# Three late expert groups instead of two in a decoder block, and a value stage written out with its weight splitting moved from GpSimd to ScalarE and VectorE

## The chip, the core and the metric

The kernel runs on one NeuronCore of a Trainium2 chip. The metric is the device time of one execution in microseconds; the median of three executions stands for a kernel. The traces are of one profiled execution.

## What is computed

A hybrid decoder block for 256 tokens of width 2048 in float32: two gated token mixers, a cross-attention to 256 memory tokens, and a product-key expert layer (PEER), with residual sums between them. The change touches only the last of these and its routing:

```python
def peer_ffn(xn, wq, sub_keys, u_tab, v_tab):
    q = (xn @ wq).reshape(B, S, PEER_HEADS, 2, PEER_HALF)
    s = jnp.einsum('bshpd,hpnd->bshpn', q, sub_keys)
    top_v, top_i = lax.top_k(s, PEER_TOPK)                 # 16 of 128, two halves
    cand = top_v[..., 0, :, None] + top_v[..., 1, None, :]  # 256 candidates
    cand_v, cand_i = lax.top_k(cand, PEER_TOPK)
    experts = i1 * PEER_NKEYS + i2                          # 16 of 16,384
    gates = jax.nn.softmax(cand_v, axis=-1)
    ...
    act = jax.nn.gelu(jnp.einsum('td,tkd->tk', xb, u_tab[eb]))
    return jnp.einsum('tk,tkd->td', gb * act, v_tab[eb])
```

There are 8 heads and 16 experts for each head and token; both tables have 16,384 rows of 2048 floats (134 MB each). The output is the final RMSNorm of the sum.

## The kernel before

The kernel is written in Bass, with one hand-written instruction stream for each engine, and semaphores between them. After the projections (up to about 1578 us of the profiled execution) the expert layer follows in three stages.

**The gather stage.** A *group* is one head for 128 tokens, so there are 16 groups (`GROUPS`); groups 0 to 7 are of the first 128 tokens. For a group VectorE first runs `route(g)`: top 16 of two rows of 128 scores, top 16 of their 256 sums, the expert numbers (`idx_all`) and the gates; ScalarE takes the exponent (`gate_exp`). GpSimd then gathers for each of the 16 experts one row of `peer_u` per token with an indirect DMA (128 x 2048 floats, 1.05 MB) into a ring of 8 (`gather_rows`), VectorE multiplies it with the token and sums (`dot_rows`, one instruction per expert), ScalarE takes the gelu (`expert_gelu`) and VectorE the product with the gate (`weigh`), which gives `w_all`. VectorE runs this as a loop: dots of group g, route of group g+3, weigh of g. In before the loop runs over g = 1 to 12, and group 13 follows alone.

**Spreading.** The output could be had by gathering `peer_v` too. The kernel rather reads the whole table once: it builds the dense matrix `spread` (16,384 experts x 256 tokens) from the weights, one *unit* of four tokens at a time (64 units): a marking of the expert's row (`row_hot`) times a marking of its column (`col_ring`) on TensorE. ScalarE builds the markings of units 0 to 31 during the gather stage (`make_unit`) and copies the product out (`copy_unit`); for units 32 to 63 VectorE makes the row marks (`mark_rows`) and GpSimd most column marks, after the last group has been weighed.

**The value stage.** 256 *steps*, each a half row block of `peer_v` (128 x 1024 floats, 0.52 MB, `v_raw`, four buffers, loaded by SyncE's queue). ScalarE rounds it to `v_hi` (two buffers), VectorE makes the rest `v_lo` (two buffers), and TensorE multiplies in 12 matmuls of 512 columns: 8 with `v_hi` (by `e_hi` and `e_lo`), then 4 with `v_lo`. `e_hi` and `e_lo` are the same split of a *batch* of `spread`, good for 8 steps; 32 batches. In before GpSimd makes them from batch 1 on (`split_weights`: a copy and a subtraction). All 12 matmuls of a step wait for `v_split`, that is for the step's `v_lo`.

**Late groups.** Some groups of the second 128 tokens are left out of `spread` (`LATE`, groups 14 and 15). Their rows of `peer_u` and `peer_v` are gathered during the value stage by GpSimd into two buffers (`late_row`); VectorE dots the 16 `u` rows and adds the 16 weighted `v` rows to `late_sum`, one row after every third step from step 32 to step 224; TensorE adds `late_sum` near the end.

Each engine runs its own code in order; what it waits for is written out as `wait_ge` on a semaphore. The names `Apart` and `Chain` are helpers for such waits; in a loop the value waited for is computed in a register.

## Time and profile before

| | |
|---|---|
| median of three executions | 3069.42 us (3069.34 to 3070.61) |
| the profiled execution | 3075.78 us, of it the span of instructions 3074.1 us |
| gather stage, 1578 to 2243 us | VectorE busy 47 of 50 us, TensorE clock 0.50 |
| spreading of units 32 to 63 | 2244 to 2297 us |
| value stage | 2303 to 3062 us; TensorE busy 47 of 50 us, VectorE 37, GpSimd 18 |
| TensorE, VectorE, ScalarE, GpSimd busy over the whole | 77%, 69%, 42%, 25% |

The times of the profiled execution are microseconds from its first instruction. The busy time of an engine in a window says how much of it the engine worked, PEclk is the granted TensorE clock (1.00 is 2.4 GHz), the DMA share is the mean busy share of the 16 DMA engines. A row of a timeline gives start, length, engine, line of the kernel, operation, and after it the idle time ahead and who ended it. The profiled execution took 6.4 us more than the median.

### The profile page before, as it was taken

To read this page: it belongs to the slowest core of one execution; us is meant where nothing else is said; L and a number is where in the kernel's file an instruction comes from. 1 tells how busy PE (TensorE), PEld (TensorE's weight loads), DVE (VectorE), ACT (ScalarE), POOL (GpSimd) and SP (SyncE) were. 2 spreads that over 40 slices of the span, in tenths; PEclk is the share of its full clock that TensorE was granted. 3 is DMA by queue.
4 is the path that set the end of the run, shared out by engine and by line. 5 is a ranking of instruction groups with operands and counts; after the bars stand their busy time and mean duration, and the time that the engine had idled before them with its cause. 6 is when DMAs were issued, how large, how long until landed. Compare 5 with 4: busy or idle time off the path is not lost. (4 is left out here: it accounts for less than half of the span.)

```text
span 3074.1 us, 44560 instructions
## 1 busy us (share of the span) xinstructions
PE 2367.7 (77%) x15833; PEld 2184.1 (71%) x15833; DVE 2112.0 (69%) x2724; ACT 1284.0 (42%) x1857; POOL 756.8 (25%) x461
## 2 busy tenths in 40 slices
PE   7999999999999999989870000122259999999998
PEld 6899999999999999989860000012248777777776
DVE  6774556666456446434589999999975777777764
ACT  4554444444444344433520000377873333333333
POOL 0000000000001001000045756656662333433320
PEclk8999999999999999999885555555589999999999
DMA  6453665445655555535467989989815887888865
GB/s 199 130 159 117 190 181 154 148 149 164 200 165 177 184 178 177 180 110 184 146 260 325 368 342 380 367 345 377 338 37 178 298 292 283 287 288 296 296 233 170
DMA packets 338990, 695.74 MB, mean 226 GB/s; under 512 B 24792, under 2 KB 266672, under 8 KB 301376
## 3 DMA queue, kind: packets, MB, share of 16 engines
q1 hardware_dynamic: 296080, 386.19, 39.8%
q0 software_dynamic: 42304, 307.25, 24.9%
q8 instruction: 69, 1.13, 0.2%
q10 hardware_dynamic: 496, 0.84, 0.1%
q14 instruction: 41, 0.34, 0.0%
HBM read 692.11 MB, written 2.10 MB: 226 GB/s over the span
## 5 line engine op out<-in xcount | busy, mean ns | idle before, releaser
L357 DVE TENSOR_TENSOR b_w_lo<-b_raw,b_w_hi 128x1024 fp32r<-128x1024 f32 x464 | 570.0, 1245 | 534.0 <-ACT b_w_hi L352 533.4
L352 ACT ACTIVATE b_w_hi<-b_raw 128x1024 fp32r<-128x1024 f32 x464 | 485.1, 1057 | 615.9 <-PE bank L375 609.3
L375 PE MATMUL bank<-b_act_hi,b_w_hi 128*128 128x256 f32 x1920 | 548.7, 286 | 12.1 <-DVE b_w_lo L357 9.2
L375 PE MATMUL bank<-b_act_lo,b_w_hi 128*128 128x256 f32 x1920 | 545.3, 284 | 0.0
L375 PE MATMUL bank<-b_act_hi,b_w_lo 128*128 128x256 f32 x1920 | 545.2, 284 | 0.0
L1886 DVE TENSOR_TENSOR b_v_lo<-b_v_raw,b_v_hi 128x1024 fp32r<-128x1024 f32 x256 | 365.9, 1435 | 237.1 <-ACT b_v_hi L1065 216.8
L1864 DVE CUSTOM_DVE_ANT_0 b_u_ring<-b_u_ring,b_xnN 128x2048 f32<-128x2048 f32 x220 | 488.5, 2286 | 5.9 <-issue 4.1
L1065 ACT ACTIVATE b_v_hi<-b_v_raw 128x1024 fp32r<-128x1024 f32 x256 | 271.6, 1061 | 484.9 <-PE bank L1452 453.5
L642 POOL DMA_INDIRECT b_u_ring<-in_peer_u,b_stage_idx x220 | 399.6, 1817 | 228.9 <-DVE b_dots L1864 155.2
L375 PEld LDWEIGHTS bank<-b_act_hi,b_w_hi 128*128 128x128 f32 x1920 | 370.6, 193 | 15.6 <-DVE b_w_lo L357 7.8
L375 PEld LDWEIGHTS bank<-b_act_lo,b_w_hi 128*128 128x128 f32 x1920 | 370.7, 193 | 0.1
L375 PEld LDWEIGHTS bank<-b_act_hi,b_w_lo 128*128 128x128 f32 x1920 | 370.5, 193 | 0.0
L375 PE MATMUL bank<-b_att_hi,b_w_hi 128*128 128x256 f32 x1280 | 365.3, 285 | 4.1 <-DVE b_att_lo L460 4.1
L375 PE MATMUL bank<-b_att_hi,b_w_lo 128*128 128x256 f32 x1280 | 363.9, 284 | 0.0
L375 PE MATMUL bank<-b_att_lo,b_w_hi 128*128 128x256 f32 x1280 | 363.9, 284 | 0.0
L1452 PE MATMUL bank<-b_v_hi,b_e_hi 128*128 128x512 f32 x1024 | 327.0, 401 | 36.6 <-DVE b_v_lo L1886 30.3
L1452 PE MATMUL bank<-b_v_hi,b_e_lo 128*128 128x512 f32 x1024 | 322.3, 396 | 0.0
L1411 PE MATMUL bank<-b_consts,b_isel_all 128*128 128x128 f32 x4 | 1.4, 442 | 374.3 <-DVE b_w_all L1870 373.0
L1452 PE MATMUL bank<-b_v_lo,b_e_hi 128*128 128x512 f32 x1024 | 276.2, 392 | 0.0
L1411 PEld LDWEIGHTS bank<-b_consts,b_isel_all 128*128 128x128 f32 x4 | 0.6, 204 | 375.4 <-DVE b_w_all L1870 373.8
L1452 PEld LDWEIGHTS bank<-b_v_hi,b_e_hi 128*128 128x128 f32 x1024 | 191.8, 191 | 94.6 <-DVE b_v_lo L1886 50.9
L375 PEld LDWEIGHTS bank<-b_att_hi,b_w_hi 128*128 128x128 f32 x1280 | 247.7, 193 | 5.0 <-issue 5.0
(307 smaller groups left out, 3879.5 us busy)
## 6 DMA issues: line engine op xcount, KB each, us to landing
b_v_raw<-in_peer_v SPq DMA_DIRECT2D x256, 512.0 KB, 4.7
b_raw<-in_w_in SPq DMA_DIRECT2D x208, 512.0 KB, 3.9
b_raw<-in_w_proj_dsa SPq DMA_DIRECT2D x32, 512.0 KB, 3.9
b_raw<-in_w_proj_gla SPq DMA_DIRECT2D x32, 512.0 KB, 3.5
b_raw<-in_w_xk SPq DMA_DIRECT2D x32, 512.0 KB, 4.4
b_raw<-in_w_out SPq DMA_DIRECT2D x32, 512.0 KB, 3.4
b_raw<-in_w_xv SPq DMA_DIRECT2D x32, 512.0 KB, 4.6
b_raw<-in_w_xq SPq DMA_DIRECT2D x32, 512.0 KB, 4.4
```

What stands on the lines that cost most here:

```text
L352: act.activation(w_hi[:, q], raw[:, UQ * c + q], ACT.Copy).then_inc(w_high, 1)
L357: dve.tensor_tensor(w_lo[:, q], raw[:, UQ * c + q], w_hi[:, q].bitcast(F32), ALU.subtract).then_inc(w_split, 1)
L375: mm = pe.matmul(proj[c][:, n], lhs, rhs, start=(q == 0 and n == 0 and k == 0 and t == 0), stop=(q == UQ - 1 and k == UK - 1 and t == 2), ...
L642: pool.indirect_dma_start(row_tile(k, early), None, u_rows, bass.IndirectOffsetOnAxis(ap=stage_idx[:, slot, k:k + 1], axis=0)).then_inc(u_ ...
L1065: act.activation(v_hi[:, n % 2], v_raw[n % 4], ACT.Copy).then_inc(sem("v_high"), 1)
L1411: mm = pe.transpose(bank[0][:, k * P:(k + 1) * P], src[:, t * P:(t + 1) * P], ident)
L1452: mm = pe.matmul(bank[4 * t + 2 * v + m], e[:, slot, i, t * P:(t + 1) * P], x[:, v, m * 512:(m + 1) * 512], start=False, stop=(last and n ...
L1864: dve.tensor_tensor_reduce(u, u, xnN[:, t], 1.0, 0.0, ALU.mult, ALU.add, dots[:, k:k + 1]).then_inc(sem("dotted"), 1)
L1886: dve.tensor_tensor(v_lo[:, n % 2], v_raw[n % 4], v_hi[:, n % 2].bitcast(F32), ALU.subtract).then_inc(sem("v_split"), 1)
```

## The change

It does seven things (the diff below has GpSimd, ScalarE, TensorE and VectorE in this order). (1) `LATE` holds three groups, 13 to 15; so the gather stage has 13 groups, and 96 late rows (48 of each table) are spread over steps 24 to 235, at distances of two or three steps (`late_at`). (2) The loops of the gather stage are written out, so that each wait is on a constant; `route` reads `sims` itself and the copy `sc` is gone; GpSimd's index copies (`stage_idx`) are gone. (3) Since the loop over g now ends at 11, `route(14)` and `route(15)` both run at g = 11. (4) ScalarE makes the marks of units 0 to 3 ahead, in groups 5 and 6 (`row_ahead`, `mark_unit`), before their weights are known; at g = 7 it then finishes 8 units. (5) ScalarE makes `e_hi` and VectorE `e_lo` for all batches; GpSimd only gathers in the value stage. (6) TensorE waits for `v_high` ahead of a step's 8 products with `v_hi`, and for `v_split` only ahead of the 4 with `v_lo`; `v_lo` has four buffers; ScalarE in turn waits that `v_lo` of two steps ago is made. (7) ScalarE's and VectorE's value stage is written out, with the late rows inside; `late_dots` and a clearing of `late_sum` are gone.

```diff
-LATE = (GROUPS - 2, GROUPS - 1)
+LATE = tuple(range(GROUPS - 3, GROUPS))
 EARLY = LATE[0]
-LATE_UNIT = 32
+STEPS = 2 * NKEYS
+PER_BATCH = 2 * BATCH
+LATE_ROWS = 2 * PTOP * len(LATE)
+LATE_STEP = 24
+MADE_AHEAD = 4
...
+    def late_at(n):
+        span = STEPS - 2 * PER_BATCH - LATE_STEP - 4
+        return [m for m in range(LATE_ROWS) if LATE_STEP + span * m // LATE_ROWS == n]
...
-        pool.wait_ge(sem("spread_copied"), UNITS)
-        first = LATE_UNIT // (2 * BATCH)
-        for b in range(1, first + 1):
-            split_weights(b, b % 2)
...
+        pool.wait_ge(sem("e_split"), 4)
+        for m in range(LATE_ROWS):
+            g, kind, k = LATE[m // (2 * PTOP)], m // PTOP % 2, m % PTOP
+            if m >= 2:
+                pool.wait_ge(sem("late_used"), m - 1)
+            pool.indirect_dma_start(late_row[m % 2], None, (u_rows, a["peer_v"][0])[kind],
+                                    bass.IndirectOffsetOnAxis(ap=idx_all[:, g * PTOP + k:g * PTOP + k + 1], axis=0)
+                                    ).then_inc(sem(f"late_landed{m % 2}"), 16)
...
+        def value_high(n):
+            act.wait_ge(v_landed[n % 4], n // 4 * 16 + 16)
+            if n >= 2:
+                act.wait_ge(sem("v_high_used"), n - 1)
+                act.wait_ge(sem("v_split"), n - 1)
+            act.activation(v_hi[:, n % 2], v_raw[n % 4], ACT.Copy).then_inc(sem("v_high"), 1)
+        def weights_high(b):
+            if b >= 2:
+                act.wait_ge(sem("v_used"), PER_BATCH * (b - 1))
+            hi, w = weights_of(b, e_hi)
+            act.activation(hi, w, ACT.Copy).then_inc(sem("e_high"), 1)
...
+            if g == EARLY - 2:
+                for late in range(g + 4, GROUPS):
+                    gate_exp(late)
-            for u in range(made, min(made + (4 if g == 7 else 6), UNITS // 2)):
+            for u in range(made, min(made + (MADE_AHEAD + 4 if g == 7 else 6), UNITS // 2)):
...
+        for n in range(STEPS):
+            value_high(n)
+            if n == 1:
+                weights_high(0)
+            if n % PER_BATCH == 2 and n // PER_BATCH + 1 < NKEYS // BATCH:
+                weights_high(n // PER_BATCH + 1)
...
-                pe.wait_ge(sem("v_split"), b * 4 * BATCH + n + 1)
+                pe.wait_ge(sem("v_high"), b * 4 * BATCH + n + 1)
                 slot, i, v = n // (2 * BATCH), n // 2 % BATCH, n % 2
-                for parts, x, done in (((e_hi, e_lo), v_hi, "v_high_used"), ((e_hi,), v_lo, "v_used")):
+                for parts, x, done in (((e_hi, e_lo), v_hi[:, v], "v_high_used"), ((e_hi,), v_lo[n % 4], "v_used")):
+                    if done == "v_used":
+                        pe.wait_ge(sem("v_split"), b * 4 * BATCH + n + 1)
...
-            link(dve.tensor_copy(sc, sims[:, bass.ds(g, 1)].rearrange("p g s n -> p (g s) n")))
-            top16(*[(tv[:, s], ti[:, s], sc[:, s], sc2[:, s]) for s in range(2)])
+            top16(*[(tv[:, s], ti[:, s], sims[:, g, s], sc2[:, s]) for s in range(2)])
...
+        for n in range(STEPS):
+            value_low(n)
+            if n == 1:
+                weights_low(0)
+            if n % PER_BATCH == 3 and n // PER_BATCH + 1 < NKEYS // BATCH:
+                weights_low(n // PER_BATCH + 1)
+            for m in late_at(n):
+                late_step(m)
```

GpSimd's program in the value stage of before, from the fifth batch on; `b_late_row` is the gathered row, `b_e_hi` and `b_e_lo` the split weights:

```order
L675 CAST b_e_hi<-b_spread 128x1024
L677 TENSOR_TENSOR b_e_lo<-b_spread,b_e_hi 128x1024
L697 DMA b_late_row_117<-in_peer_u,b_stage_idx 128x2048
L697 DMA b_late_row_118<-in_peer_u,b_stage_idx 128x2048
L675 CAST b_e_hi<-b_spread 128x1024
L677 TENSOR_TENSOR b_e_lo<-b_spread,b_e_hi 128x1024
```

The same place after the change, from the last column marks on:

```order
L664 TENSOR_SCALAR b_col_ring<-b_consts,b_turned 128x128 x72
L679 DMA b_late_row_116<-in_peer_u,b_idx_all 128x2048
L679 DMA b_late_row_117<-in_peer_u,b_idx_all 128x2048
L679 DMA b_late_row_116<-in_peer_u,b_idx_all 128x2048
L679 DMA b_late_row_117<-in_peer_u,b_idx_all 128x2048
```

Both kinds of splitting instruction have left GpSimd, and its stream holds nothing but the 96 row gathers.

VectorE in before, the loop body of the late `u` rows; `b_v_lo` is the remainder of a step's values, the two L1898 rows are one dot and its sum's read-out:

```order
L1886 TENSOR_TENSOR b_v_lo<-b_v_raw_125,b_v_hi 128x1024
L1898 ISA b_late_row_117,b_late_dots<-b_late_row_117,b_xnN 128x2048
L1898 ISA b_late_dots 128x1
L1883 REGISTER_ALU
L1886 TENSOR_TENSOR b_v_lo<-b_v_raw_126,b_v_hi 128x1024
L1883 REGISTER_ALU
L1886 TENSOR_TENSOR b_v_lo<-b_v_raw_127,b_v_hi 128x1024
L1883 REGISTER_ALU
L1886 TENSOR_TENSOR b_v_lo<-b_v_raw_128,b_v_hi 128x1024
```

VectorE after the change, from step 24 on:

```order
L1886 TENSOR_TENSOR b_v_lo_130<-b_v_raw_125,b_v_hi 128x1024
L1902 ISA b_late_row_116,b_dots<-b_late_row_116,b_xnN 128x2048
L1902 ISA b_dots 128x1
L1886 TENSOR_TENSOR b_v_lo_131<-b_v_raw_126,b_v_hi 128x1024
L1886 TENSOR_TENSOR b_v_lo_132<-b_v_raw_127,b_v_hi 128x1024
L1902 ISA b_late_row_117,b_dots<-b_late_row_117,b_xnN 128x2048
L1902 ISA b_dots 128x1
L1886 TENSOR_TENSOR b_v_lo_133<-b_v_raw_128,b_v_hi 128x1024
L1891 TENSOR_TENSOR b_e_lo<-b_spread,b_e_hi 128x1024
```

A row comes after every second step (every fifth distance or so is three), and the batch's `b_e_lo` has joined the stream once in 8 steps.

ScalarE after the change, at g = 11, the last turn in which it builds units:

```order
L1044 ACTIVATE b_gelu<-b_dots 128x16
L990 ACT_TABLE_LOAD
L990 ACTIVATE b_egate,b_stat<-b_cv,b_stat 128x16 x2
L1005 ACTIVATE b_row_hot<-b_consts,b_turned 128x128 x4
L1005 ACTIVATE b_col_ring<-b_consts,b_turned 128x128 x4
```

Where before had one exponent ahead of the last six units, there are two now, of groups 14 and 15, and the second waits for `route(15)`.

## Rows read from the trace of the kernel before

**Rows 1.** windows, a gather and a value stretch; first row: columns

```profile
core 0: us, PE busy (x) PEld busy (x) DVE busy (x) ACT busy (x) POOL busy (x), PEclk, DMA share, GB/s
1850.00:1900.00 50.00, 0.00 (x0) 0.00 (x0) 47.34 (x76) 3.18 (x5) 32.58 (x18) 0.50 0.89 358
2600.00:2650.00 50.00, 46.94 (x198) 37.73 (x197) 37.42 (x22) 17.79 (x17) 17.96 (x9) 0.97 0.84 306
```

**Rows 2.** timeline, VectorE, one gather turn: start, length (us), engine, line

```profile
1909.58 0.29 DVE L1838 COPY b_sc<-b_sims 128x256 f32 x1
...
1921.48 2.29 DVE L1864 CUSTOM_DVE_ANT_0 b_u_ring<-b_u_ring,b_xnN 128x2048 f32<-128x2048 f32 x1 [0.41 <-issue]
...
1956.89 0.28 DVE L1838 COPY b_sc<-b_sims 128x256 f32 x1
```

**Rows 3.** timeline, VectorE, route(0) outside the loop, first and last instruction

```profile
1537.71 0.29 DVE L1838 COPY b_sc<-b_sims 128x256 f32<-128x256 f32 x1
...
1547.04 0.23 DVE L1858 TENSOR_SCALAR b_gates_all<-b_egate,b_stat 128x16 f32<-128x16 f32 x1
```

**Rows 4.** timeline, the end of the gather stage, VectorE and ScalarE

```profile
2193.03 0.29 DVE L1838 COPY b_sc<-b_sims 128x256 f32 x1
...
2200.00 0.31 ACT L1010 ACTIVATE b_egate<-b_cv,b_stat 128x16 f32<-128x16 f32 x1 [5.34 <-DVE b_stat L1845]
...
2242.78 0.21 ACT L1057 ACTIVATE b_gelu<-b_dots 128x16 f32<-128x16 f32 x1
...
2243.03 0.17 DVE L1870 TENSOR_TENSOR b_w_all<-b_gelu,b_gates_all 128x16 f32<-128x16 f32 x1 [2.99 <-ACT b_gelu L1057]
```

**Rows 5.** timeline, the start of the value stage, VectorE and TensorE

```profile
2297.51 4.58 DVE L1886 TENSOR_TENSOR b_v_lo<-b_v_raw,b_v_hi 128x1024 fp32r<-128x1024 f32 x2 [3.22 <-ACT b_v_hi L1065]
...
2303.28 1.22 PE L1452 MATMUL bank<-b_v_hi,b_e_hi 128*128 128x512 f32 x2 [4.62 <-DVE b_e_lo L1943]
```

**Rows 6.** timeline, one even step of the value stage, three engines

```profile
2313.97 0.61 PE L1452 MATMUL bank<-b_v_hi,b_e_hi 128*128 128x512 f32 x2
...
2315.79 1.07 PE L1452 MATMUL bank<-b_v_lo,b_e_hi 128*128 128x512 f32 x4
...
2316.05 1.06 ACT L1065 ACTIVATE b_v_hi<-b_v_raw 128x1024 fp32r<-128x1024 f32 x1 [1.66 <-PE bank L1452]
...
2316.69 0.61 PE L1452 MATMUL bank<-b_v_hi,b_e_hi 128*128 128x512 f32 x2
...
2317.14 1.23 DVE L1886 TENSOR_TENSOR b_v_lo<-b_v_raw,b_v_hi 128x1024 fp32r<-128x1024 f32 x1 [1.50 <-ACT b_v_hi L1065]
```

**Rows 7.** timeline, a step in which GpSimd splits weights

```profile
2328.92 3.26 POOL L677 TENSOR_TENSOR b_e_lo<-b_spread,b_e_hi 128x1024 fp32r<-128x1024 f32 x1
...
2330.74 2.53 DVE L1886 TENSOR_TENSOR b_v_lo<-b_v_raw,b_v_hi 128x1024 fp32r<-128x1024 f32 x1 [0.82 <-ACT b_v_hi L1065]
```

**Rows 8.** groups, 2310:3040: count, busy us, mean ns, idle before

```profile
L1886 DVE TENSOR_TENSOR b_v_lo<-b_v_raw,b_v_hi 128x1024 fp32r<-128x1024 f32 x247 | 352.7, 1434 | 223.4 <-ACT b_v_hi L1065 203.1 <-PE bank L1452 19.8 <-DVE b_w_all L1870 0.3
```

**Rows 9.** the chain that ended last, its end: start us, length us

```profile
3015.34 3.43 PE bank L1476 x8
...
3062.34 1.84 ACT b_hN L1120 x6
```

**Rows 10.** windows of the value stage; columns as in rows 1

```profile
2312.00:2326.00 14.00, 14.00 (x64) 11.58 (x63) 6.53 (x6) 5.30 (x5) 0.00 (x0) 1.00 0.59 190
...
2400.00:2500.00 100.00, 93.86 (x400) 75.24 (x399) 74.69 (x59) 35.78 (x34) 38.35 (x20) 0.98 0.81 295
...
2525.00:2530.00 5.00, 5.00 (x24) 4.14 (x23) 4.05 (x4) 1.98 (x2) 0.34 (x1) 1.00 1.01 416
```

**Rows 11.** tile b_late_row, 2300:3040: instructions and time from issue to landing

```profile
L1902 DVE SCALAR_TENSOR_TENSOR b_late_sum<-b_late_row,b_w_all,b_late_sum x32: 2339/2346/4492, 2536.8 to 2961.4; 128x2048 f32<-128x2048 f32 x32
...
DMA to landing us min/median/max: 8.1/8.6/10.7
```

**Rows 12.** tile b_v_raw, 2400:2900: time from issue to landing

```profile
DMA to landing us min/median/max: 3.5/5.7/9.0
```

More of the change, by code:

```diff
@@ L273, in hybrid_block @@
     v_hi = sb("v_hi", [2, VCOLS], SCR, F32R)
-    v_lo = sb("v_lo", [2, VCOLS], SCR + 8 * K, F32R)
+    v_lo = [sb(f"v_lo{n}", [VCOLS], at, F32R) for n, at in enumerate((SCR + 8 * K, SCR + 12 * K, WRK, WRK + 4 * K))]
     gfin = sb("gfin", [D], HT)
@@ L700, in _ @@
-        for b in range(first + 25, NKEYS // BATCH):
-            split_weights(b, b % 2)
+        pool.wait_ge(sem("e_split"), 4)
[6 more added lines that the diff above has]
+                                    ).then_inc(sem(f"late_landed{m % 2}"), 16)
@@ L1057, in expert_gelu @@
             act.activation(gelu, dots, ACT.Gelu_apprx_tanh).then_inc(sem("gelu_ready"), 1)
-        def values_high(at, steps, first=False):
-            for n in steps:
-                act.wait_ge(v_landed[n % 4], at * 16 + (n // 4 + 1) * 16)
-                if not (first and n < 2):
-                    act.wait_ge(sem("v_high_used"), at * 4 + (n - 1))
-                act.activation(v_hi[:, n % 2], v_raw[n % 4], ACT.Copy).then_inc(sem("v_high"), 1)
+        def value_high(n):
[9 more added lines that the diff above has]
+            act.activation(hi, w, ACT.Copy).then_inc(sem("e_high"), 1)
         peer_pair(PQ, 0)
@@ L1075, in _ @@
         gate_exp(3)
-        with act.Fori(1, 8) as g:
+        for g in range(1, 8):
             expert_gelu(g)
             gate_exp(g + 3)
-        turn_over(0, (0, 3))
+            if g == 4:
+                act.wait_ge(sem("routed"), PEER_H)
+                turn_over(0, (0, 2))
+            if g in (5, 6):
+                mark_unit(2 * (g - 5))
+                mark_unit(2 * (g - 5) + 1)
+        turn_over(1, (2, 3))
         made = 0
@@ L1088, in _ @@
         copy_unit(UNITS // 2 - 1)
-        turn_over(1, (0, 2))
+        turn_over(2, (0, 2))
         act.wait_ge(sem("routed"), GROUPS)
@@ L1452, in values @@
                                 mm = pe.matmul(bank[4 * t + 2 * v + m], e[:, slot, i, t * P:(t + 1) * P],
-                                               x[:, v, m * 512:(m + 1) * 512], start=False,
-                                               stop=(last and n >= 4 * BATCH - 2 and x is v_lo), skip_group_check=True)
+                                               x[:, m * 512:(m + 1) * 512], start=False,
+                                               stop=(last and n >= 4 * BATCH - 2 and done == "v_used"), skip_group_check=True)
                     mm.then_inc(sem(done), 1)
@@ L1469, in _ @@
         pe.wait_ge(sem("spread_copied"), UNITS)
-        seed(range(2))
-        values(0, first=True)
-        with pe.Fori(1, NKEYS // (2 * BATCH) - 1) as b:
+        seed(range(2)).then_inc(sem("seeded"), 1)
+        with pe.Fori(0, NKEYS // (2 * BATCH) - 1) as b:
             values(b)
-        pe.wait_ge(sem("late_used"), 4 * PTOP)
+        pe.wait_ge(sem("late_used"), LATE_ROWS)
         for n in range(4):
@@ new lines, in value_low, with weights_low @@
+        def value_low(n):
+            dve.wait_ge(sem("v_high"), n + 1)
+            if n == 2:
+                dve.wait_ge(sem("seeded"), 2)
+            if n >= 4:
+                dve.wait_ge(sem("v_used"), n - 3)
+            dve.tensor_tensor(v_lo[n % 4], v_raw[n % 4], v_hi[:, n % 2].bitcast(F32), ALU.subtract).then_inc(sem("v_split"), 1)
+        def weights_low(b):
+            dve.wait_ge(sem("e_high"), b + 1)
+            hi, w = weights_of(b, e_hi)
+            dve.tensor_tensor(weights_of(b, e_lo)[0], w, hi.bitcast(F32), ALU.subtract).then_inc(sem("e_split"), 1)
@@ new lines, in late_step @@
+        def late_step(m):
+            g, kind, k = LATE[m // (2 * PTOP)], m // PTOP % 2, m % PTOP
+            row = late_row[m % 2]
+            if kind == 1 and k == 0:
+                weigh(g)
+                dve.wait_ge(sem("weights_ready"), g + 1)
+            dve.wait_ge(sem(f"late_landed{m % 2}"), m // 2 * 16 + 16)
+            if kind == 0:
+                dve.tensor_tensor_reduce(row, row, xnN[:, 1], 1.0, 0.0, ALU.mult, ALU.add, dots[:, k:k + 1]
+                                         ).then_inc(sem("late_used"), 1)
+                return
+            w = w_all[:, g * PTOP + k:g * PTOP + k + 1]
+            dve.wait_ge(sem("late_used"), m)
+            if m == PTOP:
+                dve.wait_ge(sem("e_split"), 8)
+                dve.tensor_scalar(late_sum, row, w, None, ALU.mult).then_inc(sem("late_used"), 1)
+            else:
+                dve.scalar_tensor_tensor(out=late_sum, in0=row, scalar=w, in1=late_sum, op0=ALU.mult, op1=ALU.add
+                                         ).then_inc(sem("late_used"), 1)
```

182 lines of the change are left out of this document (51 added, 131 removed).

## The prediction

> **What bounds the kernel now.** I read the busy windows first, to see which engine is full in which stage. In the gather stage VectorE works 47.3 of 50 us and TensorE nothing; in the value stage TensorE works 46.9 of 50 at nearly the full clock (0.97), VectorE 37.4, and the DMA engines 0.84 [rows 1]. So a VectorE instruction counts in full in the first, and only what keeps TensorE waiting counts in the second. Nothing before 1578 us is touched.
>
> The timeline of the gather stage gives the price of a turn: from one `COPY b_sc` to the next 47.3 us, of them 11.9 up to the first dot (`route`, `weigh`, the branch) and 35.4 for 16 dots, 2.21 us each [rows 2]. `route(0)`, which stands outside the loop, took 9.56 us for the same instructions [rows 3]: the loop's waits on register values cost the rest. The end of the stage is not VectorE's: its last `weigh` waited 2.99 us for ScalarE's gelu [rows 4].
>
> The value stage runs from TensorE's first product at 2303.3 [rows 5] to ScalarE's first reading of the results at 3062.3 [rows 9], 759.1 us. An even step takes 2.72 us (2313.97 to 2316.69) [rows 6]. 256 of them are 696.3; `late_sum` adds 3.4 [rows 9]; the first step runs at half pace (1.22 us for two matmuls against 0.61) and costs 2.7 more [rows 5, 6]. That makes 702.4, so TensorE loses 56.7 us to waits. The cause is in the timeline: `v_lo` takes 1.23 us alone, but 2.53 beside GpSimd's `TENSOR_TENSOR` of 3.26 us [rows 6, 7]; its mean is 1.43 over 247 [rows 8], and single late-row instructions of 2.35 us take up to 4.49 [rows 11]. All 12 matmuls of a step wait for it. In the even step `v_lo` is ready at 2318.37, and its step starts at 2319.41 (2316.69 plus 2.72): 1.0 us of slack, less than one contended instruction or one late row takes.
>
> **The change, part by part.**
>
> *Gather stage.* The 16 dots stay at 35.4 us. `route` loses the copy (0.29 us and its wait, 0.32) and runs like the one outside the loop: 9.24. With some 0.25 for `weigh` a turn is 44.9 instead of 47.3. The dots of group 12 ended at 2193.1; the last dots ahead of the same work are now those of group 11. That is one turn less (47.3) and ten turns each 2.4 shorter (24.0): 71.3 us earlier. Behind this point it gets longer. ScalarE's exponent stood at 2200.0, and from there its six units, eight column marks and the gelu ran without a gap to 2243.0, 43.0 us [rows 4]. Now two exponents stand ahead of the units, and the second waits for `route(15)`: 9.5 for `route(14)` and `weigh`, then 5.9 into `route(15)`: 15.4 us after the dots, where it was 6.9. VectorE itself would be done after 9.5 + 9.3 + 35.4 = 54.2 us, ScalarE after 15.4 + 43.0 = 58.4, against 49.9 before: 8.5 given back. The copies of `route(2)` and `route(3)` add 0.6. Net **63.4 us saved**. The marks made ahead I cost at nothing: ScalarE has 3.18 us of work in 50 in that stretch [rows 1], and in turn 7, where it now finishes eight units, it needs no longer than the 35 us of dots. Without them, turn 7 would have four full units more and ScalarE would be late by part of them.
>
> Is there another floor for the gather turn? 16 rows of 1.05 MB at the 358 GB/s of now are 46.9 us, but DMA is busy only 0.89 of the time [rows 1]; at its full pace (358/0.89 = 402) they take 41.8, under 44.9. So VectorE stays the bound, with less room.
>
> *Spreading.* Its instructions and waits stay, offset by the gelu: 0.
>
> *Start of the value stage.* The first two `v_lo` took 4.58 us beside GpSimd's split; alone they take 2.46 [rows 5, 6]. TensorE waited for what follows them: **2.1 us saved**.
>
> *Value stage.* GpSimd's splits go, so the contention goes. VectorE gets 31 more subtractions of 1.23 us and 32 more rows. In steps 24 to 235 (212 steps, 96 rows, 2.21 steps apart) its work for a step is 1.23 + 2.35/2.21 + 1.23/8 = 2.45 us of 2.72: full to 90%, yet under. What it is late by has more room: `v_lo` is now wanted only ahead of the last four matmuls, 1.81 us into the step (2313.97 to 2315.79) [rows 6], so the slack is 1.04 + 1.81 = 2.9 us. A row (2.35) fits; a row and a weight subtraction in one step put the next `v_lo` 2.1 us behind its place, and it still fits. ScalarE's extra `e_hi` (about 1.06 once in 8 steps) lies in its idle 1.66 us a step. If VectorE and ScalarE keep up, the whole 56.7 us of waits vanish. That is the one bound: nothing lost, step 2.72.
>
> The other bound is transfers. A step in that stretch moves 0.524 MB of values and 1.049/2.21 = 0.475 MB of rows, 0.999 MB in 2.72 us: 367 GB/s, where the stage now averages 295 at a DMA share of 0.81. In time: values alone hold the share at 0.59, so 1.60 us a step; the average of now (a step of 0.874 MB at 295 GB/s is 2.96 us, 0.81 of it 2.40) leaves (2.40 - 1.60) x 3 = 2.4 us a row [rows 10]. The new step needs 1.60 + 2.4/2.21 = 2.69 us of DMA in 2.72. A 5-us window in which 416 GB/s were reached in this very mix says there is a little more to have [rows 10]. The second sign is the ring of two rows: issue to use may take 2 x 2.21 x 2.72 = 12.0 us less 2.35 for the row itself and some 0.3 for waking GpSimd: 9.4 us. The landing takes 8.6 in the median, 10.7 at most [rows 11]. At 10.7 for every row the step would be (10.7 + 2.65)/4.42 = 3.02 us. A value block has four buffers, 10.9 us, of which 2.4 go for its two splits; it lands in 5.7, at most 9.0 [rows 12], and ScalarE has 2.3 us of slack beside.
>
> So the step in the late stretch lies between 2.72 and 3.02 us, 0 to 64 us over 212 steps. I take 2.80, nearer to the lower end since every mean fits and only the tails do not: **17 us given back**.
>
> At this place the Trainium skill speaks against the change: "DMA: Bandwidth & Descriptors", section "Where 436 GB/s comes from", holds that transfers from HBM are bound by some 358 GB/s per core. The 416 GB/s window and the 402 above go beyond that here. By the page the late step would be an estimated 0.999 MB / 358 GB/s = 2.79 us and the give-back 15 us; by the window's 416 it would be 2.72 and nothing.
>
> *Sum.* 63.4 + 2.1 + 56.7 - 17 = 105.2 us. The profiled execution took 3075.8 and would take 2970.6. It lies 6.4 above the median, which I carry over: **2964 us** for the median, 3.4% less.
>
> **The rivals.**
>
> *A: transfers set the pace of the late stretch.* For it: 2.69 of 2.72 us of DMA, a row ring with 0.8 us to spare over the median, and instructions that wait in order, so a late row holds up the next `v_lo`. Against it: no late row has made VectorE wait so far (the waits ahead of `v_lo` are for ScalarE and TensorE [rows 8]). Step 2.88 to 3.1, at 2.96 (the pace the stage has now): 51 us given back instead of 17, 2998 us.
>
> *B: GpSimd isn't what slows `v_lo`, or VectorE becomes the bound.* If `v_lo` kept its mean of 1.43, VectorE's step would be 2.65, with waking times some 2.85: 28 us given back, 2975. Against it: 1.23 us in every step without a GpSimd split.
>
> *C: slower than before.* If the 295 GB/s of now were already what this mix of queues yields, the step would be 0.999/295 = 3.39 us, 142 us lost in the late stretch against 2.72: 3089 us. It decides from a step of about 3.30 on, or a row landing of 11.9 us. Against it: windows of 416 and shares of 0.81, which leave idle time.
>
> *D: the gather stage gives less.* If the written-out turns kept 47.3 us (the extra time being no matter of register waits), 24 us and a little more would be missing: 2989.
>
> **How the numbers follow.** The forecast (late step 2.72 to 2.88, 2947 to 2981 us) gets 0.60, B falls in its range and gets 0.06 of its own, A 0.24, D 0.05, C 0.03, and 0.02 is for what I have not seen. The low end is the stage without any give-back, 2947, less 3 for small terms; the high end reaches over most of A and D: 2944 to 3000. A measurement of this kernel tells 0.2% (6 us) from no change. All cases but C end far below: faster 0.96, within 0.2% 0.01, slower 0.03.
>
> **What would show it.** Right: dots of group 12 begin 18.8 us after those of group 11 end, with gather turns of 44.9; ScalarE's gelu ends 4 us after VectorE's last dot; `v_lo` has a mean near 1.23; even steps of 2.72 before step 24 and after 235, and 2.75 to 2.85 between; the DMA share there over 0.93. Wrong: idle time of VectorE ahead of late rows, rows landing in over 9.4 us, ScalarE waiting for value blocks; turns over 46 us; or gaps for code that is now written out instead of looped.

## The result: 2.4% faster, at the far end of the range

| | before | after |
|---|---|---|
| median | 3070.02 us (4 runs, 3069.34 to 3075.49) | 2999.31 us (4 runs, 2990.09 to 3006.46) |
| ratio, 95% interval | | 0.9764 [0.9734, 0.9794] |
| the profiled execution | 3075.78 us | 3006.46 us |

The forecast was 2964 us, range 2944 to 3000. Sign and range hold, but the time is 35 us above the forecast and close to that of rival A (2998), in part by luck, as told below. One later execution of the changed kernel took 7326 us and enters no figure. The profiled execution of the changed kernel is the slowest of its four, 7.2 us above their median; that of before lay 6.4 above the median on which the forecast was built. The table takes both profiled executions apart in the terms of the forecast's sum. The gelu is the last one of the gather stage, the value stage is from TensorE's first product to the end of its last.

| | before | after | saved | forecast |
|---|---|---|---|---|
| gather stage, to the gelu's end | 2242.99 | 2188.11 | 54.9 | 63.4 |
| from there to the first product | 60.3 | 58.2 | 2.1 | 2.1 |
| value stage | 759.0 | 746.5 | 12.5 | 56.7 - 17 = 39.7 |
| sum | | | 69.5 | 105.2 |

The executions differ by 69.3 us, so nothing is missing. Two terms of the forecast's sum are off: the gather stage by 8.5 us, the value stage by 27.2.

### The gather stage after

VectorE's timeline (start, length, engine, line, operation), with the first and the last dot of group 11, the exponents and units of ScalarE behind it, and the last weigh; they answer to [rows 2, 4]:

```profile
2083.06 2.29 DVE L1863 CUSTOM_DVE_ANT_0 b_u_ring<-b_u_ring,b_xnN 128x2048 f32<-128x2048 f32 x1
...
2118.46 0.08 DVE L1863 DVE_READ_ACCUMULATOR2_ANT b_dots<- 128x1 f32 x1
...
2124.43 0.31 ACT L990 ACTIVATE b_egate<-b_cv,b_stat 128x16 f32<-128x16 f32 x1 [4.34 <-DVE b_stat L1844]
2133.80 0.31 ACT L990 ACTIVATE b_egate<-b_cv,b_stat 128x16 f32<-128x16 f32 x1 [8.96 <-DVE b_stat L1844]
2134.10 1.26 ACT L1005 ACTIVATE b_row_hot<-b_consts,b_turned 128x128 f32<-128x128 f32 x4
...
2139.78 1.25 ACT L1005 ACTIVATE b_row_hot<-b_consts,b_turned 128x128 f32<-128x128 f32 x4
...
2162.39 1.23 ACT L1005 ACTIVATE b_row_hot<-b_consts,b_turned 128x128 f32<-128x128 f32 x4
...
2187.89 0.22 ACT L1044 ACTIVATE b_gelu<-b_dots 128x16 f32<-128x16 f32 x1
2188.14 0.18 DVE L1869 TENSOR_TENSOR b_w_all<-b_gelu,b_gates_all 128x16 f32<-128x16 f32 x1 [15.55 <-ACT b_gelu L1044]
```

Group 11's dots end at 2118.5, where those of group 12 ended at 2193.1: 74.6 us earlier, 71.9 forecast. The second exponent begins 15.3 us behind them (15.4 worked out). But from there to the gelu it is 54.1 us and not 43.0, and VectorE stands for 15.55 us. On ScalarE a unit begins with four `b_row_hot` instructions; one begins every 5.65 us, and between 2134.10 and 2162.39 six of them do. The same place of before, the start of each unit behind the exponent of 2200.0 in [rows 4]:

```profile
2200.31 1.26 ACT L1025 ACTIVATE b_row_hot<-b_consts,b_turned 128x128 f32<-128x128 f32 x4
...
2205.96 1.24 ACT L1025 ACTIVATE b_row_hot<-b_consts,b_turned 128x128 f32<-128x128 f32 x4
...
2211.62 1.23 ACT L1025 ACTIVATE b_row_hot<-b_consts,b_turned 128x128 f32<-128x128 f32 x4
...
2217.26 1.25 ACT L1025 ACTIVATE b_row_hot<-b_consts,b_turned 128x128 f32<-128x128 f32 x4
```

There were four units in before. The prediction took them for six.

### The value stage after

Windows of the value stage (columns as in [rows 1]): before the late rows, between them, and the whole late stretch; the second answers to [rows 10]:

```profile
2252.00:2300.00 48.00, 48.00 (x214) 39.74 (x213) 24.65 (x21) 20.97 (x21) 0.00 (x0) 1.00 0.57 187
2400.00:2500.00 100.00, 95.62 (x407) 74.77 (x406) 76.22 (x55) 39.29 (x39) 25.19 (x15) 1.00 0.92 334
2304.00:2920.00 616.00, 592.69 (x2528) 469.86 (x2528) 486.20 (x382) 247.34 (x239) 162.28 (x94) 1.00 0.93 339
```

Before the late rows begin TensorE has no gap. Among them the DMA share is 0.93 at 339 GB/s, and TensorE is idle for 23.3 us by this view (the last section tells why the loss is larger than that). The groups of VectorE and the waits in the same window (total, times, longest), which answer to [rows 8, 11], and the landing time of the value blocks, which answers to [rows 12]:

```profile
L1886 DVE TENSOR_TENSOR b_v_lo<-b_v_raw,b_v_hi 128x1024 fp32r<-128x1024 f32 x211 | 252.2, 1220 | 60.7 <-ACT b_v_hi L1052 60.7
L1902 DVE CUSTOM_DVE_ANT_0 b_late_row<-b_late_row,b_xnN 128x2048 f32<-128x2048 f32 x48 | 109.9, 2289 | 36.9 <-DMA b_late_row<-in_peer_u,b_idx_all 36.6
L1911 DVE SCALAR_TENSOR_TENSOR b_late_sum<-b_late_row,b_w_all,b_late_sum 128x2048 f32<-128x2048 f32 x45 | 105.7, 2349 | 33.3 <-DMA b_late_row<-in_peer_v,b_idx_all 32.0 <-issue 1.3
```

```profile
ACT b_v_hi L1052 <- DMA b_v_raw<-in_peer_v: 290.4, 136, 4.9
...
PEld bank L1451 <- DVE b_v_lo L1886: 40.6, 54, 2.5
DVE b_late_row L1902 <- DMA b_late_row<-in_peer_u,b_idx_all: 36.6, 25, 2.9
DVE b_late_sum L1911 <- DMA b_late_row<-in_peer_v,b_idx_all: 32.0, 23, 3.7
PE bank L1451 <- DVE b_v_lo L1886: 20.0, 29, 2.1
```

```profile
DMA to landing us min/median/max: 6.1/7.9/9.2
```

The contention with GpSimd is gone: `v_lo` takes 1.22 us on the mean (1.43 before), a row never more than 2.36. What waits now waits for DMA: ScalarE for value blocks 136 times, VectorE for rows 48 times (68.6 us). One place of VectorE's and TensorE's timelines shows how a late row reaches TensorE:

```profile
2644.99 2.35 DVE L1911 SCALAR_TENSOR_TENSOR b_late_sum<-b_late_row,b_w_all,b_late_sum 128x2048 f32<-128x2048 f32 x1 [3.65 <-DMA b_late_row<-in_peer_v,b_idx_all]
2647.26 2.35 DVE L1886 TENSOR_TENSOR b_v_lo<-b_v_raw,b_v_hi 128x1024 fp32r<-128x1024 f32 x2
```

```profile
2645.81 0.61 PE L1451 MATMUL bank<-b_v_hi,b_e_lo 128*128 128x512 f32 x2
2648.53 1.49 PE L1451 MATMUL bank<-b_v_lo,b_e_hi 128*128 128x512 f32 x4 [2.11 <-DVE b_v_lo L1886]
2649.82 1.06 PE L1451 MATMUL bank<-b_v_hi,b_e_hi 128*128 128x512 f32 x2
2650.68 1.06 PE L1451 MATMUL bank<-b_v_hi,b_e_lo 128*128 128x512 f32 x2
```

VectorE stands 3.65 us for a row, the `v_lo` behind it comes late, TensorE stands 2.11 us, and its next products take 1.06 us a pair where they took 0.61.

### The profile page after: what moved, and what is told of

The parts are those of the page before. It is cut to its first block, busy times and chain, and to the rows that moved or that the text cites. A ratio compares the mean times of both kernels' runs of the same rounds, so it can differ in the third digit from the quotient of the medians.

```text
span 3004.7 us, 43116 instructions
## 1 busy us (share of the span) xinstructions
PE 2362.4 (79%) x15833; PEld 2173.8 (72%) x15833; DVE 2097.8 (70%) x2746; ACT 1309.9 (44%) x1887; POOL 635.2 (21%) x399
## 4 chain that ended last, share of the span: by engine, by line
PE 54%; DVE 24%; DMA 13%; issue 5%; ACT 4%; POOL 1%; DVEq 0%; SPq 0%; ACTq 0%; POOLq 0%
PE bank L377 42%; DVE b_u_ring L1863 13%; PE bank L1451 6%; DMA b_v_raw<-in_peer_v 5%; DMA b_late_row<-in_peer_v,b_idx_all 4%; DMA b_late_row<-in_peer_u,b_idx_all 4%; DVE b_v_lo L1886 1%; DVE b_late_sum L1911 1%; PE bank L1261 1%; PE bank L1146 1%; ACT b_spread L996 1%; ACT b_v_hi L1052 1%; DVE b_w_lo L359 1%; DVE b_rstd L421 1%; PE bank L1428 1%
## 5 line engine op out<-in xcount | busy, mean ns | idle before, releaser
L1863 DVE CUSTOM_DVE_ANT_0 b_u_ring<-b_u_ring,b_xnN 128x2048 f32<-128x2048 f32 x204 | 453.0, 2288 | 1.6 <-DMA b_u_ring<-in_peer_u,b_idx_all 1.5
L653 POOL DMA_INDIRECT b_u_ring<-in_peer_u,b_idx_all x204 | 385.3, 1888 | 245.6 <-DVE b_dots L1863 132.6
L1886 DVE TENSOR_TENSOR b_v_lo<-b_v_raw,b_v_hi 128x1024 fp32r<-128x1024 f32 x256 | 307.1, 1221 | 122.8 <-ACT b_v_hi L1052 122.8
L1451 PE MATMUL bank<-b_v_hi,b_e_hi 128*128 128x512 f32 x1024 | 320.2, 394 | 5.5 <-DVE b_e_lo L1891 2.7
L377 PEld LDWEIGHTS bank<-b_att_lo,b_w_hi 128*128 128x128 f32 x1280 | 247.5, 193 | 0.1
L377 PEld LDWEIGHTS bank<-b_att_hi,b_w_lo 128*128 128x128 f32 x1280 | 247.5, 193 | 0.0
L1451 PEld LDWEIGHTS bank<-b_v_lo,b_e_hi 128*128 128x128 f32 x1024 | 188.0, 188 | 78.7 <-DVE b_v_lo L1886 42.2
```

What stands on the lines that cost most here:

```text
L377: mm = pe.matmul(proj[c][:, n], lhs, rhs, start=(q == 0 and n == 0 and k == 0 and t == 0), stop=(q == UQ - 1 and k == UK - 1 and t == 2), ...
L653: pool.indirect_dma_start(row_tile(k, g == 0), None, u_rows, bass.IndirectOffsetOnAxis(ap=idx_all[:, at:at + 1], axis=0)).then_inc(u_lande ...
L1451: mm = pe.matmul(bank[4 * t + 2 * v + m], e[:, slot, i, t * P:(t + 1) * P], x[:, m * 512:(m + 1) * 512], start=False, stop=(last and n >= ...
L1863: dve.tensor_tensor_reduce(u, u, xnN[:, t], 1.0, 0.0, ALU.mult, ALU.add, dots[:, k:k + 1]).then_inc(sem("dotted"), 1)
L1886: dve.tensor_tensor(v_lo[n % 4], v_raw[n % 4], v_hi[:, n % 2].bitcast(F32), ALU.subtract).then_inc(sem("v_split"), 1)
```

## The experiments

All are edits of the changed kernel. The value stage's floor below is what e1 and e2 reach, where TensorE has no gap: 701.7 us. "Stage" is the value stage, always from the first product to the end of the last. The three columns of events are each from one profiled execution, which may lie some 7 us off the median of its kernel; medians and ratios to before are from all runs.

| | late groups | last gelu | first product | stage | median | ratio to before |
|---|---|---|---|---|---|---|
| after, again | 3 | 2184.6 | 2244.4 | 748.0 | 3003.7 | 0.9756 [0.9741, 0.9772] |
| e1 | 2 | 2208.7 | 2267.4 | 701.7 | 2982.6 | 0.9698 [0.9685, 0.9711] |
| e2 small rows | 3 | 2184.1 | 2242.1 | 701.7 | 2957.2 | 0.9623 [0.9606, 0.9641] |
| e3 larger ring | 3 | 2181.9 | 2240.7 | 722.1 | 2976.6 | 0.9691 [0.9678, 0.9704] |
| e4 rows to 248 | 3 | 2188.7 | 2247.1 | 717.9 | 2974.5 | 0.9675 [0.9661, 0.9688] |
| e5 tail | 3 | 2171.1 | 2232.1 | 739.3 | 2985.8 | 0.9728 [0.9715, 0.9742] |
| e8 = e3+e4+e5 | 3 | 2171.2 | 2232.1 | 708.5 | 2956.7 | 0.9632 [0.9619, 0.9646] |
| e6 GpSimd splits | 2 | 2208.5 | 2267.4 | 707.6 | 2986.5 | 0.9721 [0.9706, 0.9736] |
| e7 one wait | 2 | 2207.3 | 2265.9 | 711.3 | 2989.2 | 0.9731 [0.9716, 0.9746] |
| e10 = e6+e7 | 2 | 2208.3 | 2267.6 | 748.1 | 3029.0 | 0.9853 [0.9839, 0.9868] |
| e11 = e10, 2 buffers | 2 | 2204.8 | 2264.7 | 751.9 | 3027.5 | 0.9849 [0.9834, 0.9863] |

**The changed kernel again.** 

> The changed kernel once more, since its four times lie between 2990 and 3006 us while e3, e4 and e5 each came with one of their own: median 2990 to 3000 us, and a value stage of 735 to 747 us in the profiled execution. If it is below 2990, the gains put to e3, e4 and e5 against the first profile are too large by the difference.

Both came out a little above what was expected: median 3003.7 (five times between 2993.6 and 3006.1), stage 748.0, which is that of the first profile within 1.5 us. So the gains of e3, e4 and e5 against the first profile aren't overstated. The gelu moved by 3.3 us with the same instructions, so a few us of the column "last gelu" mean nothing: the last gelu of e3 is 6 us earlier than that of after though e3 changes nothing ahead of it. The gains below are therefore read from the stage, and from the gap between two events of one trace, and held against the medians.

**Two groups (e1).** What does the third late group bring?

```diff
-LATE = tuple(range(GROUPS - 3, GROUPS))
+LATE = tuple(range(GROUPS - 2, GROUPS))
```

> Two late groups (14 and 15) as before, all else as after the change: 64 late rows over the same 212 steps. The gather stage gets one more turn of 44.8 us on VectorE, but ScalarE then has fewer units left behind the last group: the profile of after has six units of 5.65 us and a gelu 15.6 us later than VectorE's last dot, and here I expect no such wait, so the gelu comes some 20 us later than in after, near 2208. Theory of transfers (some 340 GB/s is what value blocks and rows together get): 64 rows in 212 steps ask for 0.30 rows a step and 309 GB/s at 2.72 us a step, so the value stage falls from 746.5 to about 705 to 712 us, and the sum is about 15 to 20 us faster than after. Theory of lock step (a row is asked for only when one of two buffers is free, and VectorE, ScalarE and TensorE wait for each other at each late row, whatever the bandwidth): the loss goes by the number of rows, 64 of 96, so the value stage is about 731 us and the sum is some 5 us slower than after.

The window of the late stretch (TensorE busy for all of it):

```profile
2304.00:2920.00 616.00, 616.00 (x2720) 510.06 (x2719) 444.70 (x353) 267.56 (x257) 105.44 (x64) 1.00 0.84 302
```

The theory of transfers gave 705 to 712 for the stage, lock step 731: it is 701.7, no gap at all. The gelu is at 2208.7, as expected, and behind VectorE's last dot, not behind ScalarE. So the third group takes 21 to 24 us off the time up to the gelu and puts 45 to 46 on the value stage of the profiles: with the two row buffers and the row positions of the change it costs 17 to 21 us by the medians. The kernel with two groups is the faster one by ratio, with intervals that don't touch.

**Small rows (e2).** Each late gather brings 64 columns; the other 1984 are left out (the two row buffers are cleared once). Since the edit views the table as pieces of 64 columns, an index now picks a piece out of the first 512 rows of the table, and no longer its own row.

```diff
-            pool.indirect_dma_start(late_row[m % 2], None, (u_rows, a["peer_v"][0])[kind],
+            if m < 2:
+                pool.memset(late_row[m], 0.0).then_inc(sem("late_blank"), 1)
+                pool.wait_ge(sem("late_blank"), m + 1)
+            pool.indirect_dma_start(late_row[m % 2][:, 0:64], None, (u_rows, a["peer_v"][0])[kind].rearrange("n (a b) -> (n a) b", b=64),
```

> Each late gather brings 64 of 2048 columns of a row (0.03 instead of 1.05 MB), and VectorE's work, the number of gathers and all waits stay; what is left out is the other columns of the late rows, so the output isn't the reference's. Theory of transfers: with 100 MB fewer to move the late stretch needs no longer for a step than the others, 2.72 us, and the value stage takes 702 to 710 us instead of 746.5 (total 35 to 45 us less than after). Theory that VectorE's own work (1.23 a step and 2.3 us a row) or the chain of waits of rows is what costs: the value stage stays above 735 us.

The window, and VectorE's `v_lo` and row groups:

```profile
2304.00:2920.00 616.00, 616.00 (x2712) 508.75 (x2711) 511.40 (x401) 265.93 (x257) 158.14 (x94) 1.00 0.60 197
```

```profile
L1889 DVE TENSOR_TENSOR b_v_lo<-b_v_raw,b_v_hi 128x1024 fp32r<-128x1024 f32 x226 | 275.2, 1222 | 105.9 <-ACT b_v_hi L1055 105.9
L1914 DVE SCALAR_TENSOR_TENSOR b_late_sum<-b_late_row,b_w_all,b_late_sum 128x2048 f32<-128x2048 f32 x47 | 110.3, 2346 | 0.1
```

With the same 96 gathers, the same work on VectorE (511 of 616 us) and the same waits, but some 98 MB fewer, the stage is 701.7, and the total falls by 42 to 46 us. So all of the 45 us lost in after comes with fetching the full rows; VectorE's load, the order and the semaphores cost nothing as long as rows land early (5.0 us in the median here). Whether it is the rate or the time that one row takes to land, and what part the place of the rows in the table has, e2 can't tell.

**A larger ring (e3).** Is it the bandwidth, or that only two rows can be under way?

```diff
+LATE_BUFFERS = ((0, 0, None), (0, 64, None), (18, 72, 8), (31, 16, 12))
...
-    late_row = [sb(f"late_row{n}", [D], RAW + n * 64 * K) for n in range(2)]
+    late_row = [sb(f"late_row{n}", [D], RAW + at * K) for n, (_, at, _) in enumerate(LATE_BUFFERS)]
...
```

(A triple holds the first row that may use the buffer, its place, and how many batches of `spread` must have been split before; each row takes the buffer that was used longest ago.)

> The late rows have two buffers up to row 17, three from row 18 and four from row 31 on, in room that the spread matrix has given up by then; nothing else is changed. Lock-step theory (a gather waits 7.8 to 9.2 us for its landing, and only two can be under way or in use): most of the 44 us lost in the late stretch comes back, the step falls from 2.93 to 2.75 to 2.80 us, total 25 to 40 us less than after. Transfers theory: the same bytes at the same 340 GB/s, within 5 us of after; rows then wait landed in their buffer, and the waits of VectorE for rows turn into waits of ScalarE for value blocks.

The window, and the row groups of VectorE:

```profile
2304.00:2920.00 616.00, 605.30 (x2623) 488.79 (x2622) 501.42 (x392) 256.94 (x248) 160.69 (x94) 1.00 0.92 348
```

```profile
L1929 DVE SCALAR_TENSOR_TENSOR b_late_sum<-b_late_row,b_w_all,b_late_sum 128x2048 f32<-128x2048 f32 x47 | 110.3, 2346 | 2.9 <-DMA b_late_row<-in_peer_v,b_idx_all 2.8
L1920 DVE CUSTOM_DVE_ANT_0 b_late_row<-b_late_row,b_xnN 128x2048 f32<-128x2048 f32 x48 | 109.7, 2286 | 13.8 <-DMA b_late_row<-in_peer_u,b_idx_all 13.8
```

Neither theory is whole. The stage falls by 24.4 us, just short of what lock step gave (25 to 40), and the late step to 2.72 + (722.1 - 701.7)/212 = 2.82 us. Waits for rows fall from 68.6 to 16.6 us, and the rate rises to 355 GB/s between 2350 and 2900 (340 in after). But 20 us stay lost, with a DMA share of 0.94 in that stretch and ScalarE waiting 232 us for value blocks (290 in after, 49 in e1): what is left goes with the rate.

**The same rows over more steps (e4).**

```diff
-        span = STEPS - 2 * PER_BATCH - LATE_STEP - 4
+        span = STEPS - LATE_STEP - 5
```

(TensorE adds `late_sum` ahead of step 252.)

> The 96 late rows are spread over 227 steps, from 24 to 250, instead of 212, and TensorE adds their sum at the start of step 252 rather than after the last. Transfers theory: at 340 GB/s the same 201 MB of rows and value blocks take the same time, but the 15 steps that were at 2.72 us with DMA at .5 now carry their share: the late stretch moves 227 value blocks and 96 rows, (227 x 0.524 + 96 x 1.049) MB / 340 GB/s = 646 us against 212 steps' 623 us plus 15 x 2.72 = 664 us, so 18 us less than after. Lock-step theory (the loss goes by the number of rows): no change, within 5 us of after.

```profile
2304.00:2920.00 616.00, 608.57 (x2651) 493.97 (x2650) 493.84 (x391) 259.08 (x250) 155.91 (x92) 1.00 0.93 345
```

The stage falls by 28.6 us, not 18, to 717.9: a demand of 356 instead of 367 GB/s at full pace goes with a higher rate, 345, with the same two buffers, and waits for rows fall to 23 us (12.5 and 10.7). "No change" is refuted, and so is the fixed 340 GB/s.

**ScalarE's tail (e5).** One of the six units is made between the two exponents, where ScalarE was idle, and four of the eight kept column marks move behind the gelu.

```diff
             if g == EARLY - 2:
                 for late in range(g + 4, GROUPS):
+                    make_unit(made)
+                    made += 1
                     gate_exp(late)
...
-        for u in range(UNITS // 2, UNITS // 2 + KEPT):
+        for u in range(UNITS // 2, UNITS // 2 + 4):
```

(The four column marks that moved follow one at a time, each ahead of a copy.)

> Three groups as in the change; ScalarE makes one of the six units that stand behind the last exponent between the two exponents of g = 11, where it is idle, and four of its eight kept column marks after the gelu, between copies. Theory of the tail (VectorE waits 15.6 us for a gelu that stands behind ScalarE's six units of 5.65 us and eight column marks of 2.4 us): the gelu comes about 13 us earlier, near 2175, and all behind it too, total 8 to 13 us less than after, ratio to before near 0.972. Rival (the spread part is then bound by the marks that were moved behind the gelu): the spread part gets longer by what is won, total within 4 us of after.

The last two gelus of e5:

```profile
2114.75 0.22 ACT L1044 ACTIVATE b_gelu<-b_dots 128x16 f32<-128x16 f32 x1 [3.18 <-DVE b_dots L1867]
...
2171.13 0.21 ACT L1044 ACTIVATE b_gelu<-b_dots 128x16 f32<-128x16 f32 x1
```

They are 56.4 us apart, 69.3 in after: 12.9 us earlier, as expected. The stretch up to the first product gets 2.5 us longer (60.7), so some 10 are left. The ratio fell by 0.003 to 0.004, about 10 us. The stage is 7.2 us shorter in this one profile though no edit touches it; its late stretch moved 344 GB/s between 2350 and 2900, where both profiles of after moved 340. So the rate varies by this much from run to run, and differences of the stage below some 7 us say little by themselves.

**All three (e8).** 

> Three groups with the changed tail of e5, the larger ring of e3 and the rows spread to step 248 of e4 together. If the gains add up: e3 and e4 each left the value stage some 20 to 24 us shorter than after (746.5), of 44.9 that can be had; 227 steps at 2.72 us ask for 220 MB in 617 us, 356 GB/s, which is just what the late stretch of e3 moved (355), so the stage takes 702 to 712 us, and the tail gives 8 to 13: total 2942 to 2955. If 346 GB/s is the cap with rows that are evenly spread (e4): 635 us in place of 617, value stage near 720, total 2955 to 2962.

```profile
2304.00:2920.00 616.00, 613.32 (x2689) 502.80 (x2688) 506.68 (x397) 263.27 (x255) 154.30 (x93) 1.00 0.94 351
```

2956.7 us, 3.7% under before and 1.3% under the changed kernel; stage 708.5, in the first theory's range (702 to 712), total just above it. Only here does the third late group clearly pay (e3 and e4 alone overlap with e1 in their intervals): 20 us under e1 by the ratios, 26 by the medians, and e1's stage has no gap left that a ring could remove.

**What the splits and the waits were worth (e6, e7, e10, e11).** These run with two groups, where transfers don't disturb. e6 puts the weight splits back on GpSimd, between its gathers (its program alternates again as in before). e7 restores the one wait:

```diff
-                pe.wait_ge(sem("v_high"), b * 4 * BATCH + n + 1)
+                pe.wait_ge(sem("v_split"), b * 4 * BATCH + n + 1)
...
-                    if done == "v_used":
-                        pe.wait_ge(sem("v_split"), b * 4 * BATCH + n + 1)
```

e10 does both, and e11 gives `v_lo` two buffers as well.

> On the kernel with two late groups (e1), whose value stage ran without a wait of TensorE in 701.7 us, the weights e_hi and e_lo are made by GpSimd again, in order with its gathers; the waits of part 6 stay. Theory 1 (GpSimd's subtraction, which slows VectorE's from 1.23 to 2.5 us, is what cost the 57 us of waits): the value stage grows by 35 to 57 us. Theory 2 (what cost them was the wait of all 12 products for v_lo and its two buffers; with part 6 there is slack for slow subtractions): it grows by at most 12 us, and VectorE's subtractions are seen at 2.5 us without anyone waiting long.

> On the kernel with two late groups (e1) all 12 products of a step wait for v_lo again; its four buffers and the splits on ScalarE and VectorE stay. Theory 1 (GpSimd was the cause): the value stage grows from 701.7 by at most 10 us. Theory 2 (the wait was the cause): at a late row VectorE's 2.3 us stand between v_hi and v_lo, the products begin up to 1 us late at each of 64 rows, and the stage grows by 30 to 60 us.

> Two late groups, with both edits undone at once: the splits on GpSimd (alone they cost the value stage 5.9 us over 701.7) and the wait of all 12 products for v_lo (alone 9.6 us). Theory of separate costs: the stage takes about 717 us, and the rest of the 57.4 us of before lies elsewhere (the two buffers of v_lo, the order of the loops). Theory that each edit covered for the other (a slow subtraction of 2.5 us hurts only where the products wait for it, and the other way round): the stage takes 735 to 760 us.

> As e10, and v_lo has two buffers again, so that all of part 5 and 6 is undone and only the written-out order is left of the value stage's changes. If the two buffers mattered, the stage is over 5 us longer than that of e10; since the products of a step wait for v_lo anyway, I expect at most 5 us more, and a total near that of before's value stage (759 us) if nothing else of the change counts.

By the stage e6 costs 5.9 us and e7 9.6, both together 46.5; by the medians it is 4, 7 and 46. So each edit undone alone speaks against the theory that names it as the cause, and only both together bring the loss back: the second theory of e10. The 3.8 us that the two buffers of e11 add to the stage don't show in its median (3027.5 against 3029.0) and are within what the stage varies. The contention in e6 is as strong as in before (1439 ns in the same window), but TensorE hardly waits for it: 3.8 us of idle time in that window, where e10 has 26.1, and e10's are nearly all for `v_lo` (e6's `v_lo`, then TensorE's waits in e10: total, times, longest):

```profile
L1899 DVE TENSOR_TENSOR b_v_lo<-b_v_raw,b_v_hi 128x1024 fp32r<-128x1024 f32 x224 | 323.1, 1452 | 136.0 <-ACT b_v_hi L1067 135.3
```

```profile
PE bank L1462 <- DVE b_v_lo L1897: 24.7, 32, 2.4
```

The same event in both, a late row that GpSimd stretches to twice its length, in e6:

```profile
2424.57 4.48 DVE L1915 CUSTOM_DVE_ANT_0 b_late_row<-b_late_row,b_xnN 128x2048 f32<-128x2048 f32 x1
2428.98 0.08 DVE L1915 DVE_READ_ACCUMULATOR2_ANT b_dots<- 128x1 f32 x1
2428.98 3.65 DVE L1899 TENSOR_TENSOR b_v_lo<-b_v_raw,b_v_hi 128x1024 fp32r<-128x1024 f32 x3
```

and in e10, with TensorE behind it:

```profile
2432.49 4.49 DVE L1913 CUSTOM_DVE_ANT_0 b_late_row<-b_late_row,b_xnN 128x2048 f32<-128x2048 f32 x1
...
2438.18 1.22 PE L1462 MATMUL bank<-b_v_hi,b_e_hi 128*128 128x512 f32 x2 [2.36 <-DVE b_v_lo L1897]
2439.20 1.05 PE L1462 MATMUL bank<-b_v_hi,b_e_lo 128*128 128x512 f32 x2
```

In e6 three `v_lo` follow without a gap, because TensorE went on with the products of `v_hi` and so let ScalarE go on. In e10 TensorE stops, and with it the buffers of `v_hi`. So either half of the change, the splits off GpSimd or the later wait, removes most of the loss alone.

## Why the prediction was right, and where not

- *Gather turn, one turn less, the second exponent*: right. The dots of group 12 begin 18.6 us behind those of group 11 (18.8 forecast), and a turn takes 44.8 us (44.9). That it was the waits on register values that cost the rest of a turn in before, no run isolates. The end of the dots is 2.7 us better than worked out, about what this stage moves between runs.
- *"From there its six units, eight column marks and the gelu ran without a gap to 2243.0, 43.0 us"*: the step that failed in this stage. The 43.0 us hold four units (before made 4 + 6 + 6 + 6 + 6 + 4 in its turns from g = 7 on); the changed kernel has six there (8 + 6 + 6 + 6 + 6). Those are 2 x 5.65 = 11.3 us on top of the 8.5 given back. e5 shows that it is this chain that VectorE waits for. The prediction quoted a length from the trace with a count from the code.
- *Start of the value stage*: right, 2.1 us; the first two `v_lo` took 2.36 us.
- *"The whole 56.7 us of waits vanish"*: right in size where full rows don't stand in the way (e1 and e2: 701.7 against the 702.4 forecast). The cause was half told. GpSimd's contention and the wait for `v_lo` were named together, but the prediction let the waits go with the contention ("GpSimd's splits go, so the contention goes"); e6, e7 and e10 show that the two act together, 46.5 us of the 57.3, and that removing either is nearly enough. Not all of it was waiting either: a part was products at the lower clock behind stalls (last section). Rival B (contention not the cause, or VectorE the bound) is refuted by the 1220 ns and by e2. What is left, 759.0 against 748.1 of e10 and 751.9 of e11, isn't explained: those kernels still have the written-out order and other places of the rows, no run tells these apart, and 7 us are within what the stage varies. (ScalarE first reads results at 3059.6; the 3062.3 that the prediction calls its first reading is the first behind the last product, so the 759 us stand; and the first step cost 2.5 us more than an even one, not 2.7.)
- *"17 us given back"*: the step that failed in the value stage. Its mechanism, transfers with little room, is right; the term was mis-sized: 44 us, a late step of 2.93 us, 339 GB/s instead of the 357 that 2.80 us need. The sum put 2.69 us of DMA time against 2.72 us of step, which asks for a share of 0.99. Over the window of the late stretch no run here passed 0.94, and with two row buffers 0.93 moved only 339 GB/s: with more bytes asked for, each transfer took longer. Blocks took 7.9 us to land instead of 5.7; the trace of after has no landing times of the rows, but in e4, with the same two buffers, they are 9.4 us in the median and 11.7 at most, where the sum took 8.6 and 10.7. The forecast 2.80 is about what the larger ring gives (2.82, e3).
- *Rival A*'s mechanism is what happened, with a late step of 2.93 in its span of 2.88 to 3.1. That its time, 2998, meets the measured 2999 is luck: it gave back 51 us in the value stage where 44 were lost, and knew nothing of the 8.5 us of the gather stage. The range held by 0.7 us, since its high end was drawn to reach over most of A and D. A's sign "no late row has made VectorE wait so far" spoke against it only for a kernel that asks for a row every third step. *C* (295 GB/s as the cap) is refuted by 339 to 356. *D* is refuted by the turns, 44.8 us.
- On the rule of the Trainium skill that the prediction weighed ("DMA: Bandwidth & Descriptors", section "Where 436 GB/s comes from", some 358 GB/s for a core): no value stage here passes it, 339 to 356 GB/s in windows of 550 us and more with three groups, also where 367 was asked for; but it doesn't tell 339 from 355. The gather stage of this same kernel goes past it, with 378 GB/s in a window after the change:

```profile
1850.00:1900.00 50.00, 0.00 (x0) 0.00 (x0) 49.17 (x98) 13.04 (x28) 31.45 (x18) 0.50 0.93 378
```

## What to carry to other kernels

Before work is moved under a stage that streams from memory, work out the rate that it needs at full pace and compare it with the highest rate that this mix of transfers holds over a long window, not over 5 us: a kernel that needed 309 GB/s lost nothing, one that needed 356 lost 7 to 16 us, one that needed 367 lost 20 or 45, by the number of row buffers. Spreading the added transfers over more steps, and a buffer or two more for them, made the move pay here, together with the shorter tail of ScalarE; without them the smaller move was the faster. And where two edits aim at one stall, test each alone and both together: here either one removed over 36 of the 46 us that they share.
